# Keeping the residual h in two on-chip buffers, one of them a former v slot, instead of a store and a load per tile

## What is computed

```python
xn = rmsnorm(x); proj = xn @ w_in                   # 2816 columns
mix = concat(sliding_window_attention, hgrn2) @ w_o
h = x + mix
hn = rmsnorm(h)
# PEER: 8 heads x top 16 of 16384 experts for every token
sc = hn @ (w_q keys); eidx, gate = top-k of pairs, softmax
act = gelu(u[eidx] . hn)
y = h + sum_k (gate * act)[k] * v[eidx[k]]
y = rmsnorm(y)
```

## Time and profile before

| | |
|---|---|
| median of 3 runs | 3558.62 us (3557.82 to 3565.39) |
| the profiled execution | 3555.45 us, span 3553.6 us |
| PE busy | 2983.7 us (84%) |
| POOL busy | 2434.8 us (69%) |
| DVE busy | 2123.3 us (60%) |
| ACT busy | 1522.3 us (43%) |
| DMA | 1222.30 MB, mean 344 GB/s |
| gathers of u / v rows | 1056 / 1056, 512 KB each |

### The profile page before, as it was taken

The page is one execution under the profiler, slowest core; times in us unless marked ns, Lnnn a source line. Parts: engine busy times, 40 slices in busy tenths (PEclk is TensorE's granted clock), DMA queues, the critical chain, the costliest instruction groups (busy, mean ns, idle before and its releaser), DMA issues.

```text
span 3553.6 us, 30435 instructions
## 1 busy us (share of the span) xinstructions
PE 2983.7 (84%) x8213; PEld 1385.9 (39%) x8213; DVE 2123.3 (60%) x4852; ACT 1522.3 (43%) x4094; POOL 2434.8 (69%) x2228
## 2 busy tenths in 40 slices
PE   6989699987898689878897889689968896589966
PEld 4844246443343244324432344234423442244221
DVE  2221655584658665866577657766676668454674
ACT  2021165334643474346533653365336633353333
POOL 1211276677777777777777777777777777576886
PEclk9999899999999999989998999899999999898999
DMA  5722499999999999999999999999999999898988
GB/s 189 264 83 70 151 405 354 358 341 385 385 388 375 369 394 379 388 370 402 370 395 362 405 372 380 370 407 374 392 359 407 381 388 359 317 358 308 347 315 346
DMA packets 346900, 1222.30 MB, mean 344 GB/s; under 512 B 39931, under 2 KB 51644, under 8 KB 345564
## 3 DMA queue, kind: packets, MB, share of 16 engines
q0 software_dynamic: 314272, 1140.57, 84.1%
q1 hardware_dynamic: 23596, 66.42, 5.1%
q10 hardware_dynamic: 8864, 13.37, 1.1%
HBM read 1195.56 MB, written 25.66 MB: 344 GB/s over the span
## 4 chain that ended last, share of the span: by engine, by line
PE 45%; POOL 21%; DMA 16%; DVE 8%; issue 7%; ACT 2%; SPq 0%; POOLq 0%; ACTq 0%; DVEq 0%
PE ps L1063 23%; DMA rows<-in_peer_v,idx 14%; POOL rows L452 11%; POOL rows L462 11%; PE ps L949 7%; PE ps L819 4%; PE ps L935 3%; PE ps L787 2%; DVE rows L1462 2%; PE ps L837 2%; DMA rows<-in_peer_u,idx 1%; DVE r L1353 1%; DVE r L1346 1%; PE ps L806 1%; DVE r L1347 1%
## 5 line engine op out<-in xcount | busy, mean ns | idle before, releaser
L1063 PE MATMUL ps<-rows,diag 128*128 128x512 f32 (+1 forms) x4224 | 2075.3, 624 | 468.9 <-DMA rows<-in_peer_v,idx 290.9
L1462 DVE CUSTOM_DVE_ANT_0 rows<-rows,hn_u 128x1024 f32<-128x1024 f32 x1056 | 1272.5, 1222 | 799.3 <-DMA rows<-in_peer_u,idx 794.8
L462 POOL DMA_INDIRECT rows<-in_peer_v,idx x1056 | 1200.5, 1137 | 429.7 <-issue 245.5
L1063 PEld LDWEIGHTS ps<-rows,diag 128*128 128x128 f32 (+1 forms) x4224 | 773.1, 195 | 1619.9 <-issue 1235.0
L452 POOL DMA_INDIRECT rows<-in_peer_u,idx x1056 | 1164.6, 1103 | 341.1 <-issue 321.7
L722 ACT ACTIVATE act_g<-act_g 128x1 f32<-128x1 f32 x1056 | 212.0, 201 | 1253.2 <-DVE act_g L1462 1245.9
L728 ACT ACTIVATE diag<-ident,act_g 128x128 f32<-128x128 f32 x1024 | 411.2, 402 | 344.1 <-PE ps L1063 317.1
L724 ACT ACTIVATE act_g<-act_g,gate 128x1 f32<-128x1 f32 x1056 | 311.0, 295 | 34.3
L949 PE MATMUL ps<-w_sc,r 128*128 128x512 f32 (+1 forms) x576 | 280.2, 594 | 0.0
L482 POOL DMA_DIRECT2D rows<-in_w_in x22 | 11.9, 539 | 228.9 <-PE ps L819 218.0
L722 ACT ACT_TABLE_LOAD x124 | 159.1, 1283 | 2.2
(11 more groups left out here) (270 smaller groups left out, 2114.1 us busy)
## 6 DMA issues: line engine op xcount, KB each, us to landing
rows<-in_w_in POOLq DMA_DIRECT2D x36, 512.0 KB, 3.9
rows<-in_peer_u,idx POOLq DMA_INDIRECT x1056, 6.6
rows<-in_peer_v,idx POOLq DMA_INDIRECT x1056, 6.6
r<-proj SPq DMA_DIRECT2D x8, 1344.0 KB, 10.5
rows<-in_w_in ACTq DMA_DIRECT2D x20, 512.0 KB, 6.6
w_sc<-in_w_q_t SPq DMA_DIRECT2D x8, 1024.0 KB, 7.4
proj<-rows POOLq DMA_DIRECT2D x22, 256.0 KB, 3.9
w_o<-in_w_in POOLq DMA_DIRECT2D x10, 512.0 KB, 6.6
```

Source lines behind the costliest of these rows:

```text
L462: nc.gpsimd.indirect_dma_start(ring[:, slot, :], None, a["peer_v"], bass.IndirectOffsetOnAxis(ap=idx[g % 2][:, k:k + 1], axis=0), engine_s ...
L1063: last = nc.tensor.matmul(Y[j][0:m, :], diag[:, n % DIAGS, 0:m], ring[:, slot, 512 * j:512 * (j + 1)], start=(k == 0), stop=(k == steps_of ...
L1462: V.tensor_tensor_reduce(ring[:, slot, :], ring[:, slot, :], hn_u[:, :], 1.0, 0.0, ALU.mult, ALU.add, act_g[:, k:k + 1]).then_inc(S["dots" ...
```

## The change

`hx` becomes a list of two buffers, of which tile i uses number i mod 2: `hx_even`, of its own, and slot 12 of the ring. h stays there from its sum until y is stored. The store to and the load from `h_dram` go, with the semaphores `h_stored` and `h_back` and SP's waits for `h_ready` and `hn_ready`. The load of x of tile 1 waits until the keys in slot 12 are used up. Slot 12 leaves the v ring: 3 slots for v in tile 0, 5 later.

```diff
-V_EARLY, V_LATE = (6, 7, 12, 13), (10, 11)
+V_EARLY, V_LATE = (6, 7, 13), (10, 11)
...
-    h_dram = nc.dram_tensor("h_dram", (TOK, D), F32, kind="Internal").ap()
...
-        hx = sb("hx", [P, D])
+        hx_even = sb("hx_even", [P, D])
...
+        hx = [hx_even[:, :], ring[:, 12, :]]
+        bucket_of = hx_even[0:BUCKETS + 1, 0:SKEW]
...
                     finish(w)
                     if is_sample(f):
                         load_sample(f)
-                    if f:
-                        sp.wait_ge(S["hn_ready"], f)
-                    sp.dma_start(hx[0:ntok(f), :], a["x_sample"] if is_sample(f) else x_tiles[f]).then_inc(S["x_in"], 16)
+                    if f == 1:
+                        sp.wait_ge(S["m_kept"], 2 * PH)
+                    sp.dma_start(hx[f % 2][0:ntok(f), :], a["x_sample"] if is_sample(f) else x_tiles[f]).then_inc(S["x_in"], 16)
                     if is_sample(f):
                         sample_caches(f)
-                    sp.wait_ge(S["h_ready"], f + 1)
-                    h_at = h_dram[SEQ:TOK, :] if is_sample(f) else h_tiles[f]
-                    sp.dma_start(h_at, hx[0:ntok(f), :]).then_inc(S["h_stored"], 16)
-                    sp.wait_ge(S["h_stored"], 16 * f + 16)
                 else:
                     finish(w)
-                if g is not None:
-                    if f is not None:
-                        sp.wait_ge(S["hn_ready"], f + 1)
-                    sp.dma_start(hx[0:ntok(g), :], h_dram[SEQ:TOK, :] if is_sample(g) else h_tiles[g])\
-                      .then_inc(S["h_back"], 16)
-                    if f is not None:
-                        sp.wait_ge(S["topk_done"], f + 1)
-                        sp.dma_start(w_fin, a["norm_final"]).then_inc(S["w_fin_in"], 16)
+                if g is not None and f is not None:
+                    sp.wait_ge(S["topk_done"], f + 1)
+                    sp.dma_start(w_fin, a["norm_final"]).then_inc(S["w_fin_in"], 16)
...
                 if k == 2:
                     dve.wait_ge(S["vsum"], PICKS * w + steps_of(w))
-                    dve.wait_ge(S["h_back"], 16 * w + 16)
                     for j in range(2):
                         cols = slice(512 * j, 512 * (j + 1))
-                        last = V.tensor_tensor(hx[0:m, cols], Y[j][0:m, :], hx[0:m, cols], ALU.add)
+                        last = V.tensor_tensor(hx[w % 2][0:m, cols], Y[j][0:m, :], hx[w % 2][0:m, cols], ALU.add)
```

More of the change, by code:

```diff
@@ L204, in build @@
             qe_exp qe_ready kd_d kd_exp kd_ready kd_turned kd_kept hg_out s_new rms_root mix_ready
-            mix_turned mix_kept h_mm h_ready h_stored ssq_root hn_ready hn_turned hn_kept hn_taken
+            mix_turned mix_kept h_mm h_ready ssq_root hn_ready hn_turned hn_kept hn_taken
             sc_mm sc_kept gate_d gate_exp topk_done
-            h_back y_taken y_root y_ready y_out
+            y_taken y_root y_ready y_out
             dots diag_ready vsum own_dve own_act rows_written
@@ L253, in build @@
         table = hn[0:BUCKETS + 1, :].rearrange("p (h q) -> p h q", h=HEADS)
-        bucket_of = hx[0:BUCKETS + 1, 0:SKEW]
+        hx = [hx_even[:, :], ring[:, 12, :]]
+        bucket_of = hx_even[0:BUCKETS + 1, 0:SKEW]
         replicated = [r2[:, 0:4 * SKEW], bias[:, 0:4 * SKEW]]
@@ L277, in build @@
         x_tiles = a["x_prompt"].rearrange("(i p) d -> i p d", p=P)
-        h_tiles = h_dram[0:SEQ, :].rearrange("(i p) d -> i p d", p=P)
         y_tiles = a["y_prompt"].rearrange("(i p) d -> i p d", p=P)
@@ L338, in finish @@
                     sp.wait_ge(S["y_ready"], w + 1)
-                    sp.dma_start(a["y_sample"] if is_sample(w) else y_tiles[w], hx[0:ntok(w), :]).then_inc(S["y_out"], 16)
+                    sp.dma_start(a["y_sample"] if is_sample(w) else y_tiles[w], hx[w % 2][0:ntok(w), :]).then_inc(S["y_out"], 16)
                     sp.wait_ge(S["y_out"], 16 * w + 16)
@@ L629, in front @@
                     act.wait_ge(S["h_ready"], f + 1)
-                    own.mark(nc.scalar.activation(r2[0:n, 0:D], hx[0:n, :], ACT.Square, accum_out=ssq[0:n, :]))
+                    own.mark(nc.scalar.activation(r2[0:n, 0:D], hx[f % 2][0:n, :], ACT.Square, accum_out=ssq[0:n, :]))
                     own.settle()
@@ L740, in _ @@
                         act.wait_ge(S["y_taken"], w + 1)
-                        own.mark(nc.scalar.activation(r2[0:m, 0:D], hx[0:m, :], ACT.Square, accum_out=ssq_y[0:m, :]))
+                        own.mark(nc.scalar.activation(r2[0:m, 0:D], hx[w % 2][0:m, :], ACT.Square, accum_out=ssq_y[0:m, :]))
                         own.settle()
@@ L1259, in front @@
                         cols = slice(512 * j, 512 * (j + 1))
-                        last = V.tensor_tensor(hx[0:n, cols], F[2 + j][0:n, :], hx[0:n, cols], ALU.add)
+                        last = V.tensor_tensor(hx[f % 2][0:n, cols], F[2 + j][0:n, :], hx[f % 2][0:n, cols], ALU.add)
                     last.then_inc(S["h_ready"], 1)
@@ L1266, in front @@
                     settle()
-                    V.scalar_tensor_tensor(hn[0:n, :], hx[0:n, :], rstd[0:n, :], hn[0:n, :], ALU.mult, ALU.mult)\
+                    V.scalar_tensor_tensor(hn[0:n, :], hx[f % 2][0:n, :], rstd[0:n, :], hn[0:n, :], ALU.mult, ALU.mult)\
                         .then_inc(S["hn_ready"], 1)
@@ L1479, in finish @@
                     settle()
-                    V.scalar_tensor_tensor(hx[0:m, :], hx[0:m, :], rstd_y[0:m, :], w_fin[0:m, :], ALU.mult, ALU.mult)\
+                    V.scalar_tensor_tensor(hx[w % 2][0:m, :], hx[w % 2][0:m, :], rstd_y[0:m, :], w_fin[0:m, :], ALU.mult, ALU.mult)\
                         .then_inc(S["y_ready"], 1)
```

## The result

The changed kernel is slower: 3598.64 us (median of 9 runs, 3587.36 to 3623.95) against 3564.68 us of the kernel before in the same comparison, ratio 1.0097 (95% interval 1.0074 to 1.0119). The forecast was 3617 us within 3562 to 3690. The profiled execution took 3598.64 us, its span is 3596.8 us, 43.2 us more than that of before. The traced execution of before (3555.45 us) was 9 us faster than the median above, so differences between the two traces come out some 9 us larger than between the medians. In the changed kernel the u gathers have line 442 and the v gathers line 452.

A forecast was written before the change was run, and what follows sets the result against it. POOL's gather issue was taken as the bound in tiles 1 to 6, with the v ring in tiles 0 and 7; 0 + 27 + 25 + 6 = +58 us on 3555.45 us, plus 3.2 us to the median, gave 3617 us, range 3562 to 3690.

The forecast's parts named there:

- The bound: POOL's issue of gathers bounds tiles 1 to 6, at 2.83 us a pick; tiles 0 and 7 also the v ring.
- The rule of the Trainium skill: HBM at about 358 GB/s a core would make 7.3 MB a 20 us gain; rejected, the trace showing 410 GB/s.
- The transfers, 0: Dropping h's stores and loads in tiles 0 to 6 gains 0, with ends 0 and -19 us.
- Tile 0, +27 us: Tile 0's v ring, four slots to three, becomes the bound: 3.22 to 3.43 us a pick; ends 0 and +90 us.
- The rival with the long cycle (+90): Tile 0's slot cycle stays over 11 us, landed rows held as long as before: 3693 us in all, chance 0.10.
- Tiles 1 to 6, +25 us: Tiles 1 to 6, six v slots to five: bursts of late gathers cost POOL 25 us, ends 0 and 38.
- the count: Tiles 1 to 6: 27 places among 768 gathers late with five v slots, the largest lateness of each summing to 38 us.
- Tile 7, +6 us: Tile 7: one slot less stops POOL one pick earlier in two stands, 2.8 us each; ends 0 and 36.
- The sum: Whole kernel: 0 + 27 + 25 + 6 = +58 us on the profiled execution's 3555.45 us.

The follow-up runs named there:

- f3: Kernel before with the dot products of tiles 1 to 6 over 512 of 1024 columns, on a faster chip: 3470.82 us, ratio 0.9742.
- e9: Kernel before with the dot products of tiles 1 to 6 over 512 of 1024 columns, on the slower chip: 3669.42 us, ratio 0.9825.
- e5: Changed kernel with three v slots in tile 0 but six later, u six and seven, on the slower chip: 3758.85 us, ratio 1.0051.
- e7: Kernel before with one small POOL memset ahead of each pick of tiles 1 to 6, on the slower chip: 3733.43 us, ratio 0.9985.
- e1: Kernel before, h still stored and loaded, with slot 12 taken out of the v ring and left unused: 3607.98 us, ratio 1.0120.
- e4: Kernel before, rings untouched, with h stored five times a tile instead of once: 3588.44 us, ratio 1.0060.
- e2: Changed kernel with a u slot given to the v ring (v four, later six; u five, later seven): 3570.31 us, ratio 1.0020.
- f1: The changed kernel measured once more against the kernel before, on another chip: 3612.27 us, ratio 1.0131.
- f2: Kernel before with four small POOL memsets ahead of each pick of tiles 1 to 6, on a faster chip: 3592.05 us, ratio 1.0074.
- e8: Kernel before with tile 0's ten slots cut five for u and five for v, on the slower chip: 3733.05 us, ratio 0.9995.

## Why the prediction was right, point by point

**The bound.** Right, for the chips like the first. POOL's time adds up to the span of tiles 1 to 6 before and after. That sum alone doesn't prove it, since slow transfers could have stretched POOL's instructions; f3 and e9 do, where the time falls with no transfer touched and POOL's instructions are as long at 367 as at 398 GB/s. The rule of the Trainium skill that was weighed there (DMA: Bandwidth & Descriptors, Bandwidth, HBM at about 358 GB/s a core) is not what the gathers met on the faster chips, 398 GB/s over 2092 us. The same section of the Trainium skill says that a core whose neighbour is idle measured higher, and that each gets about 358 when both cores of an HBM domain stream; the kernel runs on one core, and the traces agree with that. On the slower chip tiles 1 to 6 ran at 356 GB/s (e5, e7), near the rule's figure, and at 367 in e9; whether HBM was the reason no run tells.

**The transfers, 0.** Right for the change within what e1 can tell, at most some 11 us. As a rule it would be wrong: e4 shows 21 us for 14.7 MB more in lumps. By that price 7.3 MB would be 10 us (an estimate), which e1 doesn't exclude.

**Tile 0, +27 us.** Measured +27.5, and 442.1 to 446.0 us in the three kernels with three slots on the faster chips against 412.1 to 417.5 in those with four or five and plain traffic. The mechanism is right; that the size fits so well is partly luck. Taken row by row from the trace after, a slot's cycle was in the mean 6.13 us to landing (forecast 6.6), 1.39 us until the row's first matmul (forecast 0.94 + 0.50), 2.02 us of matmuls (1.96), and 0.80 us until the slot's next gather (0.30): 10.34 us for a forecast of 10.30. The sum let every gather start 0.3 us after its release, but POOL waited for only 73 of 128; the slots so lay free 0.5 us longer, and the quicker landing made up for it. The rival with the long cycle (+90) failed because a row's time from gather to sum fell from 11.45 to 9.54 us: of this, landed rows stood 1.39 us before their matmuls where they had stood 2.71.

**Tiles 1 to 6, +25 us.** The mechanism is right, the size somewhat high: this is a term that was mis-sized. POOL's waits for v slots beyond 0.3 us grew from 4 us to 18 (the change), 22 (its second run) and 27 us (e1), so by 14 to 22 us. The tile times, 2194.0, 2204.3 and 2193.1 us for 2177.5, say +16 to +27 us, but e2 with no waits took 2192.7. Why the count is too high wasn't tested. Likely a gather that is late makes its neighbours early, and landings get quicker when fewer gathers are under way (mean of the v gathers 7.4 us before, 6.7 after, 6.6 with four slots).

**Tile 7, +6 us.** Failed: -3.3 us, and POOL's waits beyond 0.3 us were 52.2 us after 51.3 before. The tile took 433 to 435 us in e1 and f1 with three and five slots, but in e4, f2 and f3 with the rings of before as well, so no cost of the slot shows there. The long stand is the same:

```profile
3107.80 0.94 POOL L452 DMA_INDIRECT rows<-in_peer_v,idx  x1 [20.80 <-PE ps L1053]
```

I priced one pick lost per stand, as if POOL were the bound of that stretch. After a stand PE has five rows to sum, 9.8 us of work, while a new gather needs 8.9 us; so PE need not run dry with five slots. That is argued, not shown; with four slots tile 7 took 445.2 us.

**The sum.** +58 us forecast on the profiled execution, of which 9 are too much in tiles 1 to 6 and 9 in tile 7, and 3 us of a later start were not foreseen: 43 us. By the medians the loss was 34 us, and 49 us in the second comparison: the forecast has the direction and the main term, and is too high by 9 to 24 us.

## What to carry to other kernels

Before giving a buffer slot away for fewer transfers, ask which engine issues without rest: if it is the one that fills the ring, every late slot is lost time, and a transfer by another queue that hides beside it is worth little. Price a ring by its cycle (issue gap, landing, use, what stands between) over the number of slots, against the pace of the stage, and take the slot from the ring with the larger room: here the same 4 KB cost 0.2% from the u ring and 1.0 to 1.3% from the v ring. A DMA share near 1 did not mean that the transfers were the bound. And compare waits, not only times: with six late v slots in both, tiles 1 to 6 took 2177.5 us in one build and 2192.7 in another.

## What the runs showed of the hardware that I had not expected

- Chips differ: the same kernel took 3563 us (medians) on three and 3737 us on a fourth, with 358 GB/s in tiles 1 to 6 of e8 there against 382 in the kernel before. On that chip POOL waited 14 to 20 us a tile for slots in e8, which has the late rings of before. Why is open.
- A small POOL memset ahead of a gather cost next to nothing: it took 0.118 us, four of them 0.2 us together, and the 0.30 us gap ahead of the gather shrank to 0.15 us.

The memsets on the timeline:

```profile
1250.83 0.96 POOL L462 DMA_INDIRECT rows<-in_peer_v,idx  x1 [0.30 <-PE ps L1069]
1251.79 0.21 POOL L499 MEMSET small<- 128x1 f32 x4
1252.14 0.94 POOL L452 DMA_INDIRECT rows<-in_peer_u,idx  x1 [0.15 <-issue]
```

- DVE's dot product lengthens POOL's gather instructions: halving it took 0.10 us off each of POOL's 1536 instructions in the mean, at the same traffic, on both chips where it was run.
